# Keys and normed mixer output transposed by DMA instead of TensorE in a hybrid decoder layer

## The chip, the cores and the metric

The kernel runs on the 8 cores of one Trainium2 chip. Each core runs the same program on its own sequence and its own 16 decode requests, and the cores exchange nothing. The metric is the device time of the slowest core in microseconds (us); lower is better. TensorE is called PE, VectorE DVE, ScalarE ACT, GpSimd POOL and SyncE SP.

## What is computed

One decoder layer. Per core: 2048 prompt positions (16 tiles of 128) and 128 sample positions (one tile), model width 1024.

```
z = rmsnorm(h) @ w_in                    # columns u, v_g, q, k, v_m, o, two gates
u, vg = gelu(u), layernorm(gelu(vg))
y_gm = u * (W_s vg + b)                  # causal 128x128 mixing per head, chunks of 128
# mLSTM, 4 heads of 128, chunks of 128:
s   = (q k^T) * w_intra
num = s v + w_inter * (q C);  den = sum(s) + w_inter * (q n)
C   = dec * C + (w_end * k)^T v          # state from chunk to chunk (n alike)
y_ml = sigmoid(o) * rmsnorm(num / max(|den|, exp(-m)))
h = h + concat(y_gm, y_ml) @ w_out
h = h + square(relu(rmsnorm(h) @ w_up)) @ w_down       # width 4096
h = h + sigmoid(rmsnorm(h) @ w_gate) * (p @ w_p)
y = rmsnorm(h)
```

## The kernel before

**Tiles and groups.** The 17 tiles form nine groups: groups 0 to 3 and 5 to 8 are pairs of prompt tiles, group 4 is the sample tile alone. So "from the second pair on" covers 15 tiles. In the order of work the tiles are numbered 0 to 16, the sample tile being number 8.

**Stages of the mixer.** For each group: N normalises and transposes the input (`norm_T`, by PE up to group 4, by DMA from group 5 on), U and V make the two halves of the gMLP, P projects q, k, v, o and the gates (`stage_P`), G works out the gates, M is the mLSTM, the output projection and the residual (`stage_M`). N, U and V of a group run three groups ahead of its P, G and M. Between groups, buffers with index `d2` (keys `KT`, queries `QT`, gates `SGT`) alternate in two places.

**What stage_M does for one tile.** It (1) transposes the scaled keys back to token rows, four 128x128 transposes on PE into one PSUM bank (L1251, L1252), and multiplies them by `wend` into `ktok` (L1253); (2) makes the weights and scores, with keys and queries in feature rows; (3) multiplies scores by values, adds the part from the carried state, and updates the state with `ktok`; (4) normalises, which leaves `yml` in token rows; (5) transposes `yml`, again four on PE into PSUM (L1301, L1302), gates it into `yt` (L1304), and (6) does the output projection from `ut` and `yt`, whose result DVE adds to the residual row in SBUF. Eight early tiles are then stored in DRAM (`hscr`) and loaded again for the FFN.

**FFN and the rest.** The FFN runs in four quarters over its width (B0 to B3), each over six groups of up to three tiles. Its weights come in halves from GpSimd's DMA queue (`load_q`): w_up of the first quarter goes where w_u and w_v stood, w_down where w_m and w_o stood. After them the parked tiles are loaded and then the second quarter's weights. Its inputs are normalised by `norm_B`: the first two groups' transposes by PE, the others' by DMA, through two buffers `AB` taken by turns. The sample's state update and the last stage (C) run beside the later quarters.

**What sets the order.** The program is first listed as operations with their dependences, and a planner (`Plan.schedule`, L449) deals them to the engines: with modelled durations it takes, for each engine, the operation that can start first, and among those within 0.02 us the lowest rank. Ranks come from due times and are moved by hand-kept offsets, `MOVES` (L585): a stage, a stage on an engine, or one operation by number. Each engine then executes its list in order, and waits on semaphores. All DMA transposes are issued by SP, in order with its loads and stores (`Emit.dma`, L258; L276 is the issue itself). All computing instructions are recorded on one line, L252, so that groups are told apart by shapes and names. Nearly all SBUF tiles lie in one tensor, AR; PSUM banks are pb; the identity is IDB.

Of the kernel before, what the change touches and what calls it, by code (L numbers as in the profile page):

```python
# [7 lines left out]
AF = mybir.ActivationFunctionType  # L8
ALU = mybir.AluOpType
# [573 lines left out]


MOVES = """  # L585
B0 -569  B1/pe 15.2  B1 55.2  B2/pe 70.2  B2 52.7  B3/pe 31.8  B3 36.9  C/pe 13.2  C/dve 106.1  G0 -74.9
G2/dve -13.1  G2 -22  G3 -13.4  G4/pe 11.5  G4/act 31.6  G4 -25.1  G5/dve 2.2  G6/dve 47.4  G6 -39.7  G8/dve -15.3
G8 16.9  M0/act -52  M0 -48.5  M1/pe -7.4  M1/dve 19.4  M1 -14.6  M2/pe -3.2  M2 -14.5  M3/pe 19.2  M3/dve 4.9
M3/pool 2  M4/pe -41.2  M4 41.4  M5 -83.3  M6/pe -5.1  M6 -1.3  M7/pe 10.5  M7/act 5.8  M7/dve 6.5  M7 18.5
M8/pe -18.6  M8/act 36.3  M8 10.7  N1/dve 2.2  N1 30.7  N2 22.1  N4 -8.2  P0/act -7.4  P0 -83.9  P1/pe -2.9  # L590
P1 -15.8  P2/pe 22.8  P2 -20.1  P3/pe 21.6  P3 -40.7  P4/pe 0.8  P4 4.6  P5 -10.5  P6/pe -3.3  P6 -7.2  P7/pe -7.8
P7/act -16.5  P7 37.8  P8 59  SU/pe -15.2  SU 187.8  U3/pe -27.2  U3 17.7  U8 -4.8  V1/pe -13.9  V1 28  V2/pe -15.5
V2/dve -26.5  V2 15  V3/pe -33.1  V3 33.3  V4 -12.6  V5/pe -18.8  V5/act 21  V5 -31.6  V6 56  V7/pe -33.8  V7 -13.5
V8 175  #52 -2.7  #54 -4.2  #55 -0.4  #72 11.6  #101 -9.3  #119 -8.9  #120 -4  #144 22.6  #153 -5.2  #158 -11.1
#179 -21.3  #184 -6.5  #190 -20.8  #226 15.9  #235 -6.5  #237 -14.5  #261 -12.6  #275 -34.8  #294 -1.1  #295 -0.2
#310 4.8  #312 8.4  #316 1.8  #324 18  #332 14  #337 -10.2  #340 -3.2  #343 -6.5  #357 -11.6  #358 -19.4  #389 7.2
#415 14.6  #416 4.4  #426 -2.8  #427 -12  #432 -7.5  #443 9.1  #479 20.9  #494 -7.3  #501 1.5  #504 -4.4  #506 -7.7
#537 -13.7  #563 -5.2  #582 -2.8  #585 -8.3  #586 5.1  #591 14.5  #592 -25.8  #593 16.4  #602 -8.9  #635 45.4
#636 14.5  #661 4.8  #669 25.7  #675 12.9  #681 10.4  #696 -26.3  #732 32.4  #747 -8.5  #755 5.6  #756 4.6
#763 28.4  #766 -22.3  #780 -17.5  #781 14.2  #790 -2  #791 -3.5  #808 -3.9  #811 19.4  #821 -2.8  #844 -14.3  # L600
#858 9.8  #873 28.2  #909 -19.4  #912 20.1  #919 -4.1  #921 -8.4  #923 -5.9  #925 -22.8  #934 -8.6  #939 -35.3
#940 14.2  #953 -5.3  #978 -30.6  #999 14.9  #1001 -8.6  #1026 7.1  #1028 0.7  #1071 -30  #1072 -3.5  #1075 17.7
#1078 3.6  #1080 12.3  #1083 -21.1  #1085 21.8  #1088 -13.1  #1092 33.2  #1102 6.3  #1107 -10.7  #1110 6
#1112 -15.3  #1113 -21.1  #1122 16.4  #1134 -13.5  #1136 -7.5  #1173 -15.8  #1181 -26.7  #1200 -1.8  #1202 2.6
#1204 1.6  #1205 -3  #1207 17.1  #1213 -0.9  #1215 -4.6  #1225 -17.1  #1231 -2.4  #1232 1.4  #1236 -0.4  #1247 4.1
#1254 -3  #1268 19.9  #1292 16  #1296 9.9  #1297 23.1  #1316 6.5  #1330 -25.5  #1337 18.4  #1340 -25  #1390 -15.6
#1399 2.1  #1420 -5.4  #1421 -4.5  #1434 -6.9  #1436 35.6  #1439 13.6  #1446 9.7  #1448 -29.9  #1450 -7.5
#1456 18.5  #1461 10.6  #1480 -6.4  #1486 16.7  #1491 20.6  #1495 -2.5  #1549 19.2  #1558 -1.5  #1562 -5.9
#1571 13.8  #1642 -15.4  #1667 39  #1717 62.2  #1753 -28.9  #1807 -10.3  #1825 28.6  #1852 9.3  #1855 -19
#2054 79.2  #2070 -7.6  #2083 23  #2115 -33.1  #2118 12.1  #2189 -21.1  #2198 -15.6  #2322 29.9  #2477 44.4  # L610
#2521 28.5  #2523 8.5  #2525 -19  #2538 22.6  #2555 -15.4  #2557 -14.7  #2617 128.9  #2621 73.4  #2663 33.3
#2703 42.9  #2757 43.2  #2759 65.2  #2781 -3.2  #2799 13.4  #2801 17.5  #2825 58.9  #2838 41.1  #2865 -35.9
#2881 30.5  #2901 27.1  #2923 18.3  #2940 -12.3  #2977 -39.5  #2999 -83.9  #3001 37.8  #3006 -35.4  #3023 118
#3048 -9.3  #3050 -55  #3065 -116.3
"""

DM = 1024
# [9 lines left out]
def build():  # L627
# [35 lines left out]
    with ExitStack() as st:  # L663
# [9 lines left out]
        def psb(cls):  # L673
            return V(PT(cls), PBB[0][:, :], True)
# [12 lines left out]
        def act(out, in_, func, bias=None, scale=None, accum=None):  # L687
            kw = dict(out=out, in_=in_, func=func)
            if bias is not None:
                kw["bias"] = bias  # L690
            if scale is not None:
                kw["scale"] = scale
            if accum is not None:
                kw["accum_out"] = accum
            cost = 0.17 + _nelem(in_) / 1200.0 + 0.09 * nptr(bias, scale) + (0.19 if accum is not None else 0)
            return P.add("act", [("activation", kw)], aps(in_, bias, scale), aps(out, accum), cost, tset=FN.get(func))
# [25 lines left out]
        def stt(eng, out, in0, scalar, in1, op0, op1):  # L722
            return P.add(eng, [("scalar_tensor_tensor", dict(out=out, in0=in0, scalar=scalar, in1=in1, op0=op0,
                                                             op1=op1))],
                         aps(in0, scalar, in1), [out], vcost(eng, _nelem(out), 1, nptr(scalar)))
# [43 lines left out]
        def trs(items):  # L769
            calls, reads = [], []  # L770
            for (o, i_, d_) in items:
                calls.append(("transpose", dict(out=o, in_=i_, identity=d_)))
                reads += [i_, d_]
            return P.add("pe", calls, reads, [items[0][0]], (0.056 if _dsize(items[0][1].dtype) == 2 else 0.109) * len(items))
# [89 lines left out]
        AT[0] = A.bf(8 * 256, k8(8))  # L864
        UT[3] = A.bf(4 * 256, h4)
        UT[0] = A.bf(4 * 256, h4)
        SGT, QT, KT = [[A.bf(4 * 256, h4) for _ in range(2)] for _ in range(3)]
        VAUG = [A.bf(4 * 130, h4)[:, :, 0:129] for _ in range(4)]
        BIG = [A.f32(512, h4) for _ in range(2)]
        STB = [A.bf(512, h4) for _ in range(2)]  # L870
# [72 lines left out]
        def vaug(t):  # L943
            return VWS[:, :, 0:129] if t["ty"] else VAUG[t["n"] % 4]
# [101 lines left out]
        def feat(nm, at, n, fin):  # L1046
            for hp in range(2):
                w, o_ = win(nm, hp)
                p = ps("P")
                for hh in range(2):  # L1050
                    mm(p[:, hh * n:(hh + 1) * n],
                       [(w[:, kc, o_ + hh * 128:o_ + hh * 128 + 128], at[:, kc, 0:n]) for kc in range(8)])
                fin(p[:, 0:2 * n].rearrange("p (h t) -> p h t", h=2), slice(hp * 2, hp * 2 + 2))
# [51 lines left out]
        def stage_P(gi):  # L1105
            grp = GROUPS[gi]
            n = len(grp) * 128
            at = AT[gi % NAT]
            d2 = gi % 2
            pg = ps("P")  # L1110
            mm(pg[0:64, 0:n], [(WGT[:, kc, :], at[:, kc, 0:n]) for kc in range(8)])
            feat("o", at, n, lambda p, hs: act(SGT[d2][:, hs, 0:n], p, AF.Tanh, scale=0.5))
            for j, t in enumerate(grp):
                cp("act", vaug(t)[:, :, 0:128], tokm("m", at, j).rearrange("p (h d) -> p h d", h=4))
            feat("q", at, n, lambda p, hs: cp("act", QT[d2][:, hs, 0:n], p))
            feat("k", at, n, lambda p, hs: act(KT[d2][:, hs, 0:n], p, AF.Copy, scale=QK_SCALE))
            return pg

        def stage_G(gi, pg):
# [119 lines left out]
        def stage_M(gi, gs):  # L1239
# [4 lines left out]
            for j, t in enumerate(grp):  # L1244
# [1 line left out]
                tk = slice(j * 128, (j + 1) * 128)  # L1246
                wint, emt, wend = ex[:, j, 0, :], ex[:, j, 1, :], ex[:, j, 2, :]
                big = BIG[n % 2]
                va, kt, qt = vaug(t), KT[d2], QT[d2]
                ktok = KTOK[n % 2] if ty == 0 else KTOKS[:]  # L1250
                pk = psb("M")  # L1251
                trs([(pk[:, h * 128:(h + 1) * 128], kt[:, h, tk], IDB[:]) for h in range(4)])  # L1252
                tt("dve", ktok, pk[:, 0:512].rearrange("p (h d) -> p h d", h=4),  # L1253
                   wend.unsqueeze(2).to_broadcast([128, 4, 128]), ALU.mult)
                pc = ps("M").rearrange("p (h t) -> p h t", h=4)
                mmx([(pc[:, h, :], OH[:, h, :], r3[:, tk], True, True) for h in range(4)])
                tt("dve", big, pc, MSK[:, ty, :].unsqueeze(1).to_broadcast([128, 4, 128]), ALU.add)
                for h in range(4):
                    act(big[:, h, :], big[:, h, :], AF.Exp, bias=aat[:, j, h:h + 1])
                psc = ps("M").rearrange("p (h t) -> p h t", h=4)  # L1260
                mmx([(psc[:, h, :], kt[:, h, tk], qt[:, h, tk], True, True) for h in range(4)])
                stb = STB[n % 2]
                tt("dve", stb, psc, big, ALU.mult)
                num, qcs = NUM[n % 2], QCS[n % 2] if ty == 0 else QCSS
# [11 lines left out]
                if ty == 0:  # L1276
# [21 lines left out]
                tt("pool", rq, tq, NEGH[:, 0:4], ALU.pow)  # L1298
                yml = YML[n % 2]
                tt("dve", yml, num[:, :, 0:128], rq.unsqueeze(2).to_broadcast([128, 4, 128]), ALU.mult)  # L1300
                py = psb("M")  # L1301
                trs([(py[:, h * 128:(h + 1) * 128], yml[:, h, :], IDB[:]) for h in range(4)])  # L1302
                yt = yml
                stt("dve", yt, SGT[d2][:, :, tk], 1.0, py[:, 0:512].rearrange("p (h t) -> p h t", h=4),  # L1304
                    ALU.add, ALU.mult)
                for nn in range(2):
                    cs = slice(nn * 512, (nn + 1) * 512)
                    ph = ps("M")
# [316 lines left out]
```

How the kernel before makes its waits and increments, by code:

```python
    def _emit_waits(self, eng, toks):  # L229
        for t in toks:
            if t.key[0] == "d":
                sem, val = self._sem(t.key), t.val
            else:
                sem, val = self._eng_sem_val(t.key[1], t.val)
            self.prog[eng].append(lambda e, sem=sem, val=val: e.wait_ge(sem, val))
# [13 lines left out]
        def run(e, calls=calls, sem=sem):  # L249
            ins = None
            for (name, kw) in calls:
                ins = getattr(e, name)(**kw)
            ins.then_inc(sem, 1)
# [4 lines left out]
    def dma(self, eng, kw, out, in_, after=()):  # L258
        deps, rr, wr = self._deps_for([in_], [out], "dma")
        deps += after
        i = self.dma_i[eng]
        self.dma_i[eng] += 1
        skey = ("d", eng, i % NDMASEM)
        prev = self.dma_last.get(skey)
        if prev is not None:
            deps.append(prev)
        self._emit_waits(eng, self._waits(eng, deps))
        val = self.dma_cnt.get(skey, 0) + 16
        self.dma_cnt[skey] = val
        sem = self._sem(skey)
        clock = dict(self.knows[eng])
        clock[skey] = val
        tok = Tok(skey, val, clock)
        self.dma_last[skey] = tok
        self.prog[eng].append(
            lambda e, out=out, in_=in_, sem=sem, kw=kw: e.dma_start(out=out, in_=in_, **kw).then_inc(sem, 16))
        self._record(rr, wr, tok, "dma")
        return tok
```

## Time and profile before

| | |
|---|---|
| median of 3 runs | 892.16 us (890.17 to 940.5) |
| profiled execution | 891.83 us |
| its span, slowest core | 890.3 us (cores: 880.0 to 890.3) |
| mean granted PE clock, that core | 0.989 |
| PE / DVE / ACT / POOL busy | 96% / 61% / 45% / 23% |

The span runs from the first to the last instruction of the core. A matmul's listed duration is that from its start to its result, and neighbours overlap; PE's time per matmul is the distance between starts.

### The profile page before, as it was taken

To read this page: it belongs to the slowest core of one execution; us is meant where nothing else is said; L and a number is where in the kernel's file an instruction comes from. 1 tells how busy PE (TensorE), PEld (TensorE's weight loads), DVE (VectorE), ACT (ScalarE), POOL (GpSimd) and SP (SyncE) were. 2 spreads that over 40 slices of the span, in tenths; PEclk is the share of its full clock that TensorE was granted. 3 is DMA by queue.
4 is the path that set the end of the run, shared out by engine and by line. 5 is a ranking of instruction groups with operands and counts; after the bars stand their busy time and mean duration, and the time that the engine had idled before them with its cause. 6 is when DMAs were issued, how large, how long until landed. Compare 5 with 4: busy or idle time off the path is not lost.

```text
span 890.3 us, 16667 instructions; the slowest of 8 cores (880.0 to 890.3 us)
## 1 busy us (share of the span) xinstructions
PE 856.0 (96%) x5650; PEld 513.1 (58%) x5650; DVE 539.9 (61%) x1080; ACT 398.4 (45%) x776; POOL 203.5 (23%) x312
## 2 busy tenths in 40 slices
PE   3989999999999999889999999999999999999995
PEld 2658666877677755445655555655556545455452
DVE  5858787486876884454544445755544544665566
ACT  2866567766675654351221121211122244645454
POOL 4334224425443242110010000211000011312211
PEclk9999999999999999989999999999999999999999
DMA  8995234125123079851192011682102523432322
GB/s 195 205 182 98 96 119 108 49 49 119 25 49 61 8 116 261 136 103 66 48 142 49 1 48 48 103 181 78 35 24 35 107 50 77 125 89 81 89 69 95
DMA packets 66821, 80.57 MB, mean 91 GB/s; under 512 B 43132, under 2 KB 45440, under 8 KB 65458
## 3 DMA queue, kind: packets, MB, share of 16 engines
q0 software_dynamic: 13648, 32.71, 21.9%
q1 hardware_dynamic: 53090, 46.80, 18.8%
q8 instruction: 47, 0.77, 0.4%
q14 instruction: 36, 0.29, 0.1%
HBM read 81.23 MB, written 18.12 MB: 112 GB/s over the span
## 4 chain that ended last, share of the span: by engine, by line
PE 86%; DMA 6%; ACT 2%; issue 2%; SPq 1%; DVE 1%; POOL 1%; POOLq 0%; ACTq 0%; DVEq 0%
PE pb L252 86%; DMA AR<-AR 3%; ACT AR L252 2%; DMA AR<-w_down 1%; SPq L276 1%; DVE AR L252 1%; DMA AR<-w_u 1%; DMA AR<-xp 1%; POOL SMALL L252 1%; ACT L252 0%; POOLq L283 0%; DVE SMALL L252 0%; ACTq L235 0%; DVEq L235 0%; SPq L235 0%
## 5 line engine op out<-in xcount | busy, mean ns | idle before, releaser
L252 PE MATMUL pb<-AR 128*128 128x512 bf16 (+6 forms) x5280 | 842.2, 320 | 10.2 <-DVE AR L252 6.5
L252 PEld LDWEIGHTS pb<-AR 128*128 128x128 bf16 (+2 forms) x5280 | 488.9, 99 | 343.9 <-issue 24.5
L252 ACT ACTIVATE AR<-pb 128x384 f32<-128x384 f32 (+4 forms) x356 | 171.8, 494 | 372.5 <-PE pb L252 306.5
L252 DVE TENSOR_TENSOR AR<-AR,pb 128x512 f32<-128x512 f32 (+3 forms) x226 | 132.6, 591 | 122.6 <-PE pb L252 122.0
L252 DVE TENSOR_TENSOR AR<-AR 128x384 bf16<-128x384 f32 (+7 forms) x257 | 136.0, 533 | 109.4 <-ACT AR L252 100.7
L252 ACT ACTIVATE AR<-AR 128x1024 bf16<-128x1024 f32 (+7 forms) x178 | 114.2, 674 | 65.4 <-DVE AR L252 35.3
L252 POOL TENSOR_TENSOR SMALL<-SMALL,NEGH 128x1 f32<-128x1 f32 (+1 forms) x102 | 70.1, 691 | 43.2 <-DVE SMALL L252 33.2
L252 POOL TENSOR_SCALAR SMALL<-SMALL 128x1 f32<-128x1 f32 x84 | 25.3, 301 | 236.8 <-ACT AR L252 206.7
L252 ACT ACTIVATE AR<-AR,SMALL 128x1024 bf16<-128x1024 f32 (+1 forms) x61 | 63.1, 1043 | 28.9 <-POOL SMALL L252 20.2
L252 DVE TENSOR_TENSOR AR<-pb,AR 128x258 f32<-128x258 f32 (+3 forms) x86 | 47.6, 580 | 17.2 <-PE pb L252 14.3
L252 POOL TENSOR_TENSOR AR<-AR 128x512 bf16<-128x512 f32 (+2 forms) x37 | 44.6, 1210 | 53.8 <-ACT AR L252 48.7
L252 DVE SCALAR_TENSOR_TENSOR AR<-AR,pb 128x512 f32<-128x512 f32 (+1 forms) x51 | 34.7, 684 | 31.0 <-PE pb L252 26.9
L252 POOL TENSOR_TENSOR AR<-KTOKS,CPK 128x1024 bf16<-128x1024 bf16 x8 | 15.3, 1912 | 163.7 <-PE pb L252 163.7
L252 DVE TENSOR_TENSOR AR<-AR,CPK 128x1024 bf16<-128x1024 bf16 (+3 forms) x29 | 25.4, 877 | 20.4 <-DMA AR<-AR 20.2
L252 DVE TENSOR_TENSOR AR<-pb,CPK 128x512 f32<-128x512 f32 (+2 forms) x33 | 29.7, 912 | 10.0 <-PE pb L252 9.8
L252 PE MATMUL pb<-IDB,AR 128*128 128x128 bf16 x272 | 23.5, 225 | 11.9 <-DVE AR L252 11.8
L252 POOL CAST AR<-AR 128x256 bf16<-128x256 f32 (+1 forms) x33 | 19.3, 586 | 51.5 <-DMA o_Cs<-AR 20.6
L252 PEld LDWEIGHTS pb<-IDB,AR 128*128 128x128 bf16 x272 | 18.9, 100 | 15.8 <-issue 12.6
L252 ACT ACT_TABLE_LOAD x20 | 25.7, 1283 | 3.9 <-PE pb L252 2.3
L252 DVE SCALAR_TENSOR_TENSOR AR<-AR,SMALL 128x1024 f32<-128x1024 f32 (+1 forms) x17 | 21.3, 1255 | 8.7 <-POOL SMALL L252 8.6
L252 ACT ACTIVATE AR<-pb,AR 128x129 f32<-128x129 f32 (+1 forms) x68 | 20.3, 368 | 12.9 <-PE pb L252 12.8
L252 DVE SCALAR_TENSOR_TENSOR AR<-AR 128x1024 f32<-128x1024 f32 (+3 forms) x27 | 24.5, 910 | 1.8 <-DVE AR L252 0.5
(72 smaller groups left out, 198.5 us busy)
## 6 DMA issues: line engine op xcount, KB each, us to landing
AR<-w_up POOLq DMA_DIRECT2D x8, 1024.0 KB, 11.1
AR<-w_down POOLq DMA_DIRECT2D x8, 1024.0 KB, 11.4
y_p<-AR SPq DMA_DIRECT2D x15, 512.0 KB, 2.6
hscr<-AR SPq DMA_DIRECT2D x8, 512.0 KB, 3.9
AR<-xp SPq DMA_DIRECT2D x4, 1024.0 KB, 5.2
AR<-hscr SPq DMA_DIRECT2D x8, 512.0 KB, 6.9
AR<-sC SPq DMA_DIRECT2D x8, 512.0 KB, 4.9
o_Cs<-AR SPq DMA_DIRECT2D x8, 512.0 KB, 3.5
```

What stands on the lines that cost most here:

```text
L252: ins = getattr(e, name)(**kw)
L276: lambda e, out=out, in_=in_, sem=sem, kw=kw: e.dma_start(out=out, in_=in_, **kw).then_inc(sem, 16))
```

## The change

For groups 1 to 8 the keys are transposed by one DMA of 128x512 into `ktok`, which DVE then multiplies in place by `wend`. The output `yml` is transposed by another DMA into the place of the tile's keys, and gated there. The key buffer holds each tile's keys in one run (tile, head, position), where before the two tiles of a pair lay side by side within each head. Group 0 stays on PE. The list of priority offsets is replaced as a whole (its first lines stand below).

```diff
 MOVES = """
-B0 -569  B1/pe 15.2  B1 55.2  B2/pe 70.2  B2 52.7  B3/pe 31.8  B3 36.9  C/pe 13.2  C/dve 106.1  G0 -74.9
...
+B1/pe 41.2  B1 111  B2/pe 76.6  B2 90.7  B3/pe 43.2  B3/dve -52  B3 21.6  BN1 453.9  C/pe 3.2  C/dve -57.6  C 20.3
...
-        SGT, QT, KT = [[A.bf(4 * 256, h4) for _ in range(2)] for _ in range(3)]
+        SGT, QT = [[A.bf(4 * 256, h4) for _ in range(2)] for _ in range(2)]
+        KT = [A.bf(4 * 256, ("p (j h t) -> p h j t", dict(j=2, h=4))) for _ in range(2)]
...
-            feat("k", at, n, lambda p, hs: act(KT[d2][:, hs, 0:n], p, AF.Copy, scale=QK_SCALE))
+            feat("k", at, n, lambda p, hs: act(KT[d2][:, hs, 0:n // 128, :], p.rearrange("p h (j t) -> p h j t", t=128),
+                                               AF.Copy, scale=QK_SCALE))
...
-                va, kt, qt = vaug(t), KT[d2], QT[d2]
+                va, kt, qt = vaug(t), KT[d2][:, :, j, :], QT[d2]
                 ktok = KTOK[n % 2] if ty == 0 else KTOKS[:]
-                pk = psb("M")
-                trs([(pk[:, h * 128:(h + 1) * 128], kt[:, h, tk], IDB[:]) for h in range(4)])
-                tt("dve", ktok, pk[:, 0:512].rearrange("p (h d) -> p h d", h=4),
-                   wend.unsqueeze(2).to_broadcast([128, 4, 128]), ALU.mult)
+                if gi:
+                    dma(ktok, kt.rearrange("p h t -> p (h t)"), transpose=True)
+                    ksrc = ktok
+                else:
+                    pk = psb("M")
+                    trs([(pk[:, h * 128:(h + 1) * 128], kt[:, h, :], IDB[:]) for h in range(4)])
+                    ksrc = pk[:, 0:512].rearrange("p (h d) -> p h d", h=4)
+                tt("dve", ktok, ksrc, wend.unsqueeze(2).to_broadcast([128, 4, 128]), ALU.mult)
...
-                py = psb("M")
-                trs([(py[:, h * 128:(h + 1) * 128], yml[:, h, :], IDB[:]) for h in range(4)])
-                yt = yml
-                stt("dve", yt, SGT[d2][:, :, tk], 1.0, py[:, 0:512].rearrange("p (h t) -> p h t", h=4),
-                    ALU.add, ALU.mult)
+                if gi:
+                    ysrc = yt = kt
+                    dma(yt, yml.rearrange("p h d -> p (h d)"), transpose=True)
+                else:
+                    py = psb("M")
+                    trs([(py[:, h * 128:(h + 1) * 128], yml[:, h, :], IDB[:]) for h in range(4)])
+                    ysrc, yt = py[:, 0:512].rearrange("p (h t) -> p h t", h=4), yml
+                stt("dve", yt, SGT[d2][:, :, tk], 1.0, ysrc, ALU.add, ALU.mult)
```

## Rows read from the trace of the kernel before

**Rows 1.** The page: the span, and busy time of each engine

```profile
span 890.3 us, 16667 instructions; the slowest of 8 cores (880.0 to 890.3 us)
...
PE 856.0 (96%) x5650; PEld 513.1 (58%) x5650; DVE 539.9 (61%) x1080; ACT 398.4 (45%) x776; POOL 203.5 (23%) x312
```

**Rows 2.** Waits of PE, whole run: us in total, times, longest us

```profile
PE pb L252 <- DVE AR L252: 21.3, 9, 10.9
```

**Rows 3.** Waits of PE from 49 to 310 us

```profile
PE pb L252 <- DVE AR L252: 2.8, 2, 2.6
```

**Rows 4.** Timeline of PE, three stretches: start us, us, operation, count, idle before

```profile
208.63 0.39 PE L252 MATMUL pb<-IDB,AR 128*128 128x128 bf16 x4
208.86 3.05 PE L252 MATMUL pb<-AR 128*128 128x129 bf16 x36
...
329.45 28.28 PE L252 MATMUL pb<-AR 128*128 128x384 bf16 x152
...
380.70 24.58 PE L252 MATMUL pb<-AR 128*128 128x384 bf16 x123 [5.77 <-DVE AR L252]
```

**Rows 5.** The chain that ended last, in order of time: start us, us

```profile
49.04 123.76 PE pb L252 x1085
...
318.88 12.42 DMA AR<-w_down
...
343.30 9.03 DMA AR<-AR
...
369.44 9.79 DMA AR<-AR
```

**Rows 6.** Windows, PE: us, busy (instructions), granted clock, DMA share, GB/s

```profile
170.00:180.00 10.00, 9.81 (x88) 1.00 0.29 54
350.00:360.00 10.00, 9.82 (x58) 1.00 1.09 159
376.00:381.00 5.00, 0.30 (x2) 0.67 0.61 83
381.00:384.00 3.00, 3.00 (x11) 0.50 0.09 5
```

**Rows 7.** Groups, shapes apart: PE's transposes (busy us, mean ns, idle before)

```profile
L252 PE MATMUL pb<-IDB,AR 128*128 128x128 bf16 x272 | 23.5, 225 | 11.9 <-DVE AR L252 11.8
```

**Rows 8.** Groups, shapes apart: keys by weights, output scaled, gating, power

```profile
L252 POOL TENSOR_TENSOR SMALL<-SMALL,NEGH 128x4 f32<-128x4 f32 x17 | 18.4, 1087 | 31.6 <-DVE SMALL L252 31.5
...
L252 DVE SCALAR_TENSOR_TENSOR AR<-AR,pb 128x512 bf16<-128x512 bf16 x17 | 11.6, 684 | 3.7 <-PE pb L252 3.7
L252 DVE TENSOR_TENSOR AR<-AR,SMALL 128x512 bf16<-128x512 f32 x17 | 11.6, 681 | 1.6 <-POOL SMALL L252 1.6
...
L252 DVE TENSOR_TENSOR AR<-pb,AR 128x512 bf16<-128x512 bf16 x16 | 10.8, 686 | 2.1 <-PE pb L252 1.4 <-ACT AR L252 0.5
```

**Rows 9.** L276, SP's issues: ns min/median/max; then SP's timeline near 330 us

```profile
L276 SPq DMA_TRANSPOSE AR<-AR x51: 1168/1233/6755, 113.9 to 860.1; - x51
...
326.85 2.14 SPq L276 DMA_TRANSPOSE AR<-AR  x1
335.29 6.75 SPq L276 DMA_TRANSPOSE AR<-AR  x1
```

**Rows 10.** DMA transposes, us to landing: 130 to 160 us, 165 to 250, 310 to 360

```profile
AR<-AR SPq DMA_TRANSPOSE x2, 5.2
...
AR<-AR SPq DMA_TRANSPOSE x4, 3.1
...
AR<-AR SPq DMA_TRANSPOSE x5, 9.6
```

**Rows 11.** DVE's timeline, last tile's output scaled and gated: start us, us

```profile
327.63 0.68 DVE L252 TENSOR_TENSOR AR<-AR,SMALL 128x512 bf16<-128x512 f32 x1
...
329.72 0.69 DVE L252 SCALAR_TENSOR_TENSOR AR<-AR,pb 128x512 bf16<-128x512 bf16 x1 [0.33 <-PE pb L252]
```

**Rows 12.** POOL's timeline: the first half of w_down is issued

```profile
307.23 0.83 POOL L276 DMA_DIRECT2D AR<-w_down  x1 [3.59 <-PE pb L252]
```

More of the change, by code:

```diff
@@ L585 @@
 MOVES = """
-B0 -569  B1/pe 15.2  B1 55.2  B2/pe 70.2  B2 52.7  B3/pe 31.8  B3 36.9  C/pe 13.2  C/dve 106.1  G0 -74.9
[L587 to L614, printed above, removed]
+B1/pe 41.2  B1 111  B2/pe 76.6  B2 90.7  B3/pe 43.2  B3/dve -52  B3 21.6  BN1 453.9  C/pe 3.2  C/dve -57.6  C 20.3
+G0 -100.2  G1/act -9.3  G1/dve 55.9  G1 -20.8  G2/pe -10.3  G2/act -36.3  G3 -85.7  G4 -41.4  G6/dve -13.4  G6 -5.8
@@ new lines @@
+G7/act -54.1  G7/dve -22.4  G7 27.4  G8/dve -13.1  M0/pe -14.3  M0 -14.3  M1 -27.2  M2 -47.9  M3/pe 19.1
+M3/act -15.5  M3 16.3  M4/pe -42.9  M4/dve 23  M4 22.7  M5 -161.4  M6/act 9.9  M6 -16.7  M7/pe 23.4  M7/act -11.2
+M7 33.3  M8/pe 36.5  M8/dve 5.6  M8 16.5  N1/dve -24.5  N1 31.5  N7/dve 29.6  N7 -16.7  P0 -41.4  P1/pe -0.9
+P1 -4.3  P2/pe 13.2  P2 -21.9  P3/pe -2.9  P3 -19  P4/pe 18.8  P4 16.7  P5/pe 31.2  P5 21.7  P6/pe 31.1  P7 44.5
+P8 28.4  SU 108.9  U3/pe 11.2  U3 62.2  U4 44.7  U5/pe 15.4  U6/pe -11.5  U6/act 6.3  V0 -46.1  V1/pe -11.5  V1 3.7
@@ new lines @@
+V2/pe -6.8  V2 3.4  V3/pe 2.5  V3/dve 76.7  V3 51.1  V4 76.6  V5/pe -2.2  V5 -3.8  V6 120.2  V7/dve -11.5  V7 -45.6
+V8 78.7  #55 -7.7  #60 37.3  #96 -6.3  #97 -3.4  #120 5.5  #125 23.7  #153 24.8  #173 -12  #195 7.6  #222 -6.3
+#226 8.6  #286 33.8  #288 -16.1  #292 -29.2  #294 25.7  #318 41.7  #325 -34  #357 -0.8  #364 1.6  #365 -12.7
+#394 15.3  #412 31.7  #413 12.9  #416 9.8  #423 3.3  #429 12.3  #432 -11.9  #444 -40.9  #445 3.5  #447 -42.7
+#480 22.3  #496 -8.8  #497 -10  #513 -2.8  #514 -10.7  #522 -2.9  #523 -17.1  #557 35.5  #559 8.6  #588 -15.5
@@ new lines @@
+#590 13.9  #593 -6.9  #617 29.1  #620 -6.4  #622 -14.9  #645 14.4  #647 13.8  #658 15  #659 -40.3  #661 12.8
+#670 -22.2  #681 7.6  #687 29.7  #699 34.9  #727 -13.1  #738 15  #747 -0.4  #758 14  #760 -7  #765 -9.9  #766 -8.3
+#771 -0.2  #776 -17.9  #782 -22.3  #787 43.2  #790 11.1  #797 16.3  #819 10.9  #822 11  #828 -36.4  #841 15.3
+#860 59.6  #869 17.8  #887 -22.6  #892 -20.9  #905 17.2  #920 7.4  #922 -5.4  #923 -8.4  #926 -4.9  #930 13
+#931 8.9  #933 -15.2  #934 -1.5  #936 -15  #937 -15  #939 -11  #940 -5.3  #944 -6.8  #957 13.2  #960 -28.2
@@ new lines @@
+#961 -8.4  #967 4.9  #1001 -23.7  #1022 6.1  #1069 7.1  #1071 -9.6  #1076 -3  #1083 -10.2  #1085 -15.1  #1088 5
+#1092 -8.3  #1110 -6.4  #1111 -8.1  #1173 -12.6  #1205 -3.1  #1210 14.3  #1212 -5.7  #1216 7.2  #1219 5.3
+#1225 10.3  #1234 21.4  #1299 -12.3  #1332 -20.6  #1336 -19.9  #1343 32  #1358 -23.2  #1359 22.9  #1361 -10.9
+#1364 21.5  #1380 -23.7  #1381 -12.1  #1385 -6.3  #1414 -21.6  #1425 20  #1442 16.7  #1445 14.5  #1452 15.2
+#1453 -5.3  #1454 22.6  #1459 6.1  #1461 -15.3  #1466 -15.2  #1475 19  #1479 20.5  #1489 25.7  #1495 5.9  #1501 21
@@ new lines @@
+#1505 1.3  #1517 12.6  #1518 6.4  #1526 22.6  #1544 13.1  #1590 -29.9  #1626 43.1  #1633 3.3  #1650 -36.4
+#1665 81.5  #1667 -23.8  #1717 46.3  #1867 30.7  #1890 20.9  #1986 25.6  #2014 32  #2039 53.5  #2058 48.8
+#2095 12.1  #2158 23.6  #2201 64.4  #2217 37.6  #2276 11.2  #2407 42  #2409 -23.3  #2439 21.7  #2449 13.5
+#2482 -5.8  #2487 -23.1  #2518 -48.7  #2519 -33.1  #2521 -14.1  #2523 48.8  #2527 79.7  #2538 -53.6  #2541 53.1
+#2557 34.4  #2561 10.7  #2563 6.1  #2577 -22.2  #2599 11.5  #2637 9.5  #2640 50.4  #2661 7.5  #2665 72.5
@@ L615 @@
+#2699 -10.2  #2701 -4.5  #2719 -102.7  #2721 31.9  #2739 -5.2  #2745 -49.5  #2751 -6.7  #2765 25.9  #2781 -68
+#2783 -21.7  #2805 -40.5  #2825 -57.1  #2847 3.3  #2861 -15.6  #2879 6.5  #2885 10.7  #2923 -52.6  #2925 -50.8
+#2929 -83.3  #2979 87.4  #3001 -6.2  #3005 -68.7  #3021 18.4  #3026 34.6  #3046 -81.1  #3061 -5.3
 """
@@ L1260, in stage_M @@
                 psc = ps("M").rearrange("p (h t) -> p h t", h=4)
-                mmx([(psc[:, h, :], kt[:, h, tk], qt[:, h, tk], True, True) for h in range(4)])
+                mmx([(psc[:, h, :], kt[:, h, :], qt[:, h, tk], True, True) for h in range(4)])
                 stb = STB[n % 2]
```

## The prediction

> **What bounds the kernel now.** I read the page first. TensorE (PE) is busy for 856.0 of 890.3 us, and no other engine passes 61% [rows 1]. So 34.3 us of PE idleness are all that better overlap could give, and beyond that only less PE work helps. The waits of PE say where the idleness is: 21.3 us behind VectorE (DVE) in nine places, the longest of 10.9 us at the very start, where DVE makes the identity; the rest of the 34.3 is the loads at the start and the tail after PE's last matmul [rows 2]. In the 261 us from 49 to 310 us, which hold nearly all of the mixer, PE waits for DVE only 2.8 us [rows 3]. The mixer is therefore bound by PE's stream of instructions: what leaves that stream there leaves the time, as long as nothing arrives late. The one gap inside the run that matters is the passage from mixer to FFN: PE stands still for 5.77 us before 380.70, released by DVE [rows 4]. The chain of waits shows what was late there [rows 5]: a half of w_down lands at 318.88 + 12.42 = 331.3, the parked tiles are loaded, and then three DMA transposes of normed FFN tiles, 9.0 to 9.8 us each (the first and the last stand there), follow one behind the other, because two buffers (AB) serve them by turns. DMA is jammed there: its share is 1.09 from 350 to 360 us [rows 6].
>
> **The removed PE work.** From group 1 on there are 15 tiles; each loses four transposes of the keys and four of the normed output, 120 of the 272 transposes of 128x128 bf16 in the whole run [rows 7]. What one costs has two ends. The group's busy time gives 23.5 / 272 = 0.086 us. But a listed matmul has a mean of 225 ns and overlaps its neighbours, so I take the pitch: four start at 208.63 and the next work starts at 208.86 [rows 4]. That is 0.23 us for four, 0.056 to 0.058 us each; other such pairs in PE's timeline stand 0.22 us apart, so I use 0.225. 30 groups of four by 0.225 = **6.75 us** off PE; by busy time it would be 120 x 0.086 = 10.4 us. I take 6.75, since the pitch shows when the next matmul really began; below, the end is 0, if PE merely waits as much longer. Their weight loads lie beside matmuls and count as nothing extra.
> The Trainium skill, "VectorE: DVE Perf Modes", section "The three transpose paths", gives a TensorE transpose of this size 390 ns and the DMA's crossbar 1309 ns, and its "Rules for kernel authors" say to use TensorE wherever a PSUM destination will do, as it would here: a rule against this change. By its 390 ns, the estimated relief would be 46.8 us; the rows' pitch says a seventh of that. The rule enters as the last rival.
>
> **DVE.** No operation is removed. The multiply of the keys by their weights read PSUM at 686 ns and now reads SBUF; its like, the multiply of the mixer output with both sources in SBUF, takes 681 ns. The gating operation with PSUM takes 684 ns [rows 8]; without it I bound the change by 681 and 686, so 0 to within 0.1 us over 30 instructions. Both now have two SBUF sources, which could hold up GpSimd or be held up by it; the nearest thing on POOL is the power of four numbers, 1.09 us each [rows 8]. At worst once per tile, 15 x 1.09 = 16 us of delay, at best none; DVE is busy 61% and PE works on other tiles, so I put 0 on the path.
>
> **The added DMAs.** 30 transposes of 128x512, all from SyncE's queue. One occupies that queue for at least 1.17 us, median 1.23, and at most 6.76 us, in the jam of the passage [rows 9]. All 51 of before include sizes of half and double the new one, so the new ones take some 30 x 1.23 = 37 us of queue. The mixer's nine groups fill PE from 49.0 to 329.5 us [rows 4, 5], 31 us each, 248 us for groups 1 to 8: room enough, since the other issues there are few tens. For the engines: from 170 to 180 us the share is 0.29 and the traffic 54 GB/s [rows 6], which is two 128x1024 transposes and hardly anything else (0.54 MB), so 1.45 us of all 16 engines each and 0.73 for half the size. 30 x 0.73 = 22 us over 248, nine points of share on top of a low load outside the weight loads.
> The Trainium skill, "Advanced Engine Details and Errata", section "X-Bar Transpose (TRN2)", expects 350 to 400 GB/s and transposes as fast as plain DMAs. By that the estimated load is about half, 10 us in place of 22. The row has 0.256 MB in 1.45 us, some 180 GB/s, and decides.
>
> **The added latency.** A transpose takes 3.1 us from issue to landing in a quiet stretch, 5.2 where it meets other traffic, and 9.6 in the passage [rows 10]. Before, the way over PE cost less: the last tile's output is scaled at 327.63 + 0.68 and gated at 329.72, 1.4 us later [rows 11]. So a tile's output projection comes 2 us later at rest and up to 8 us later in a jam.
> Keys: they are ready long before their use in the state update, and the transpose is not in the chain of the state; 0. Outputs: the front of the work runs three groups ahead, so PE has projections of other tiles to do; the 2.8 us of waits in 261 say that such work is never short [rows 3]. I put 0 there for groups 1 to 7, with 15 x 2 = 30 us as the far end if each tile waited. If that cover is gone, nothing but the last group remains, and there the cover ends: group 8 (tiles 15 and 16 in order of work) has no further group behind it, only FFN work on early tiles.
> Waits on SP: what queues behind a transpose waiting for the scaled output are stores of parked tiles, loads of x and later transposes of normed inputs, none wanted for tens of us, except at the end: the eight loads of parked tiles. They wait for w_down's landing at 331.3 anyway [rows 5]; the last output is ready at 328.3. Margin: 3.0 us, against a normal hold of 1.23. I take 0, and 6.76 for one held hard.
> Buffers: the output takes over the keys' place, which is then free one output projection later. Its next writer is the key projection two groups on; a group takes some 31 us; 0. The key layout is only an address pattern; 0. Freed PSUM banks can only help; 0.
>
> **The passage.** Its chain starts with w_down, whose first half is issued at 307.23 when PE has done its last use of the room [rows 12], the second at 318.88 [rows 5], behind the power of tile 15 in POOL's order. Both follow PE's progress, and by then 28 of 30 groups of transposes are gone: the chain starts 6.3 us earlier. So I let the gap stay at 5.8 and the gain pass through.
>
> **New priorities.** They move every start, and the trace of before can't price them. PE idleness in the mixer leaves at most 2.8 us to win; the passage 5.77 us, and the clock behind it: granted 0.67 from 376 to 381 and 0.50 from 381 to 384 [rows 6], where PE worked at 1.2 instead of 2.4 GHz, at 0.50 for 3 us, so 1.5 us of work lost. Together 7.3 can be won there. As much can be lost by a like gap elsewhere. I take 0.
>
> **Sum.** The profiled execution took 891.83 us, 1.5 more than its span; 891.8 - 6.75 = 885.1. The median of before, 892.16, lies 0.3 above the profiled run: 885.4.
>
> **Rivals.**
> 1. *The passage closes as well.* FFN normalisation of the second group gets its own late place, which may free ACT and AB for the tiles that were late; PE's gap and the half clock go. 885.4 - 7.3 = 878. For it: three serial 9 us transposes are a matter of order. Against: DMA is full there, and order moves no bytes.
> 2. *The gain is absorbed.* PE reaches the passage 6.75 us earlier but the tiles wait for DMAs that don't come earlier, or the added latency at the tail of the mixer eats it. 892. For it: the chain there is DMA. Against: its start is released by PE.
> 3. *Slower: SyncE's queue jams at the tail.* The output transposes of tiles 15 and 16 meet the load of w_down and hold the queue 6.76 us each, and the loads of parked tiles stand behind them. 2 x 6.76 = 13.5, less the 6.3 by which the chain starts earlier = 7.2 later than before; the gap is longer and the clock falls for longer (another 1.5): 892.2 + 8.7 = 901. It decides from a hold of more than 3.0 us for the last one. For it: holds of 6.75 appear from 335 us on. Against: at 326.85 one still went through in 2.14 [rows 9].
> 4. *The way over DMA is too long for every tile*: a 2 us wait of PE at each of 15 tiles, 30 us less 6.75, gives 885.4 + 30 = 915. For it: the added latency of 2 us is certain. Against: PE's waits of 2.8 us in the mixer [rows 3]. This is what following the rule of "VectorE: DVE Perf Modes" in the Trainium skill would avoid.
> That the change doesn't do what it says is also possible: the added DMAs could leave PE's order such that removed transposes had filled time in which it waited for DVE anyway; this is case 2 by another way.
>
> **Chances.** Forecast (881 to 889) 0.49, passage closed 0.16, absorbed 0.19, queue jam 0.12, too slow 0.04. The range reaches below the closed passage and short of the jam's full price, 876 to 900, which leaves out about 2 in 10. A change of 2%, 17.8 us, is about what a measurement of this kernel tells from none. Below 874.3 would need the closed passage and more: 0.04. Above 910 needs case 4 or a doubled jam: 0.05. Within: 0.91.
>
> **What would show it.** PE's transposes drop from 272 to 152 and its busy time by 7 to 10 us; DMA transposes rise from 51 to 81; PE's waits from 49 to 310 us stay below 5 us; the gap before the third FFN group stays 4 to 8 us with a dip of the clock behind it; DVE's groups keep 680 to 690 ns; landing of transposes in the mixer is near 3 us outside the loads. The forecast is wrong if PE's waits in the mixer exceed 7 us, if a wait of PE ends on a new DMA transpose at the tail, or if the gap before the FFN's third group changes by more than 4 us.

## The result: no faster, 0.23% slower, and the profile after

Over 20 runs each the changed kernel takes 893.9 us (median) against 891.54; the ratio is 1.0023, 95% interval 1.0014 to 1.0032. The forecast was 885.4, a gain of 0.76%. The gain is absent and the sign is the other one. Some runs of every kernel are slower by several per cent, with a lower clock on some of the cores; the medians count them, the ratios don't.

The page of the changed kernel, against [rows 1]: PE has 7.9 us less to do, and the span is not shorter.

```profile
span 891.2 us, 16401 instructions; the slowest of 8 cores (881.7 to 891.2 us)
...
PE 848.1 (95%) x5464; PEld 508.5 (57%) x5534; DVE 538.6 (60%) x1080; ACT 399.8 (45%) x778; POOL 205.2 (23%) x312
```

Groups with shapes apart, against [rows 7, 8]: PE's transposes, the gating from SBUF, the keys by their weights from SBUF.

```profile
L252 PE MATMUL pb<-IDB,AR 128*128 128x128 bf16 x152 | 12.9, 232 | 12.0 <-DVE AR L252 12.0
...
L252 DVE SCALAR_TENSOR_TENSOR AR<-AR 128x512 bf16<-128x512 bf16 x15 | 10.2, 681 | 0.0
L252 DVE TENSOR_TENSOR AR<-AR 128x512 bf16<-128x512 bf16 x14 | 9.4, 689 | 2.9 <-DMA AR<-AR 2.9
```

So 120 transposes left PE and DVE pays nothing for its new operands. PE's waits from 49 to 310 us are another matter; before there were 3.0 us, 2.8 of them behind DVE [rows 3], now 7.5, more than the 7 at which the prediction calls itself wrong:

```profile
PE pb L252 <- DVE AR L252: 3.1, 1, 3.1
PE pb L252 <- ACT AR L252: 3.0, 1, 3.0
PE pb L252 <- POOL AR L252: 0.8, 2, 0.4
PE pb L252 <- issue: 0.6, 3, 0.2
```

PE's timeline says where, and that PE still stands still in the passage from mixer to FFN, now in three pieces of together 6.2 us instead of one of 5.77 [rows 4]:

```profile
64.08 12.49 PE L252 MATMUL pb<-AR 128*128 128x129 bf16 x120 [3.03 <-ACT AR L252]
...
303.82 4.22 PE L252 MATMUL pb<-AR 128*128 128x129 bf16 x20 [3.13 <-DVE AR L252]
...
356.56 4.08 PE L252 MATMUL pb<-AR 128*128 128x384 bf16 x16 [2.22 <-DVE AR L252]
...
381.50 4.44 PE L252 MATMUL pb<-AR 128*128 128x384 bf16 x16 [2.33 <-DVE AR L252]
387.63 12.90 PE L252 MATMUL pb<-AR 128*128 128x512 bf16 x63 [1.69 <-DVE AR L252]
```

The new one in the mixer is the wait before 303.82. The chain in order of time leads through a DMA transpose to a DVE operation; DVE's timeline has there the keys' multiply of the last tile:

```profile
293.03 9.86 DMA AR<-AR
302.89 0.03 issue
302.94 0.04 issue
302.98 0.70 DVE AR L252
303.68 0.14 issue
303.82 1.45 PE pb L252 x12
```

SyncE's timeline: four transposes (the keys of tiles 15 and 16, the outputs of 13 and 14) hold its queue for 19 us, while POOL issues the first half of w_down.

```profile
288.28 19.09 SPq L276 DMA_TRANSPOSE AR<-AR  x4
```

```profile
292.28 0.83 POOL L276 DMA_DIRECT2D AR<-w_down  x1 [1.84 <-PE pb L252]
```

The transposes' us to landing, first from 60 to 285 us, then from 286 to 310:

```profile
AR<-AR SPq DMA_TRANSPOSE x31, 2.8
...
AR<-AR SPq DMA_TRANSPOSE x4, 7.6
```

And the windows of PE (stretch, its length, busy us and instructions, granted clock, DMA share, GB/s): the stretch with the wait has a mean granted clock of 0.66 where the one before it has 1.00. From 304 to 310 us, right behind the wait, PE is at work at 0.50, so the 3.1 us cost more than themselves.

```profile
290.00:300.00 10.00, 9.55 (x102) 1.00 0.66 98
300.00:310.00 10.00, 6.59 (x29) 0.66 1.07 133
```

### The profile page after: what moved, and what is told of

Read it like the earlier page. It is cut to its first block, busy times and chain, and to the rows that moved or that the text cites. A ratio compares the mean times of both kernels' runs of the same rounds, so it can differ in the third digit from the quotient of the medians.

```text
span 891.2 us, 16401 instructions; the slowest of 8 cores (881.7 to 891.2 us)
## 1 busy us (share of the span) xinstructions
PE 848.1 (95%) x5464; PEld 508.5 (57%) x5534; DVE 538.6 (60%) x1080; ACT 399.8 (45%) x778; POOL 205.2 (23%) x312
## 4 chain that ended last, share of the span: by engine, by line
PE 82%; DMA 11%; issue 2%; POOL 2%; ACT 2%; DVE 1%; SPq 0%; POOLq 0%; ACTq 0%; DVEq 0%
PE pb L252 82%; DMA AR<-AR 6%; DMA AR<-xp 3%; ACT AR L252 2%; DMA AR<-xs 1%; DVE AR L252 1%; POOL SMALL L252 1%; DMA CPK<-cpk 1%; POOL AR L276 0%; POOL AR L252 0%; SPq L276 0%; POOLq L283 0%; POOL CPK L276 0%; ACTq L235 0%; POOLq L235 0%
## 5 line engine op out<-in xcount | busy, mean ns | idle before, releaser
L252 PE MATMUL pb<-AR 128*128 128x256 bf16 (+6 forms) x5210 | 835.3, 320 | 21.9 <-DVE AR L252 9.8
L252 PEld LDWEIGHTS pb<-AR 128*128 128x128 bf16 (+1 forms) x5280 | 490.9, 99 | 354.7 <-issue 31.8
L252 ACT ACTIVATE AR<-pb 128x384 f32<-128x384 f32 (+6 forms) x356 | 172.1, 494 | 362.2 <-PE pb L252 285.0
L252 DVE TENSOR_TENSOR AR<-AR 128x384 bf16<-128x384 f32 (+9 forms) x271 | 140.7, 524 | 105.6 <-ACT AR L252 99.1
L252 ACT ACTIVATE AR<-AR 128x1024 bf16<-128x1024 f32 (+6 forms) x178 | 113.8, 675 | 89.0 <-DVE AR L252 51.8
L252 DVE TENSOR_TENSOR AR<-pb,AR 128x512 bf16<-128x512 f32 (+3 forms) x72 | 38.5, 559 | 13.9 <-PE pb L252 12.8
L252 DVE SCALAR_TENSOR_TENSOR AR<-AR,pb 128x512 f32<-128x512 f32 (+1 forms) x36 | 24.5, 684 | 23.1 <-PE pb L252 22.5
L252 DVE SCALAR_TENSOR_TENSOR AR<-AR 128x1024 f32<-128x1024 f32 (+4 forms) x42 | 34.7, 827 | 1.4
L252 PE MATMUL pb<-IDB,AR 128*128 128x128 bf16 x152 | 12.9, 232 | 12.0 <-DVE AR L252 12.0
L252 DVE SCALAR_TENSOR_TENSOR AR<-AR,DECBS,pb 128x128 f32<-128x128 f32 x64 | 19.9, 343 | 1.8 <-PE pb L252 1.8
```

The costliest lines, as they stand in the source:

```text
L252: ins = getattr(e, name)(**kw)
```

## The experiments

Each is given as its ratio to the kernel of before, run beside it on the same chip, with the 95% interval.

**The list and the transposes apart.** Two runs exchange the lists of offsets, `MOVES`; one puts group 8 back on PE and one leaves the transposes out, and both are planned anew.

```diff
e1_old_list:        the change, MOVES of before
e2_new_list_alone:  before, MOVES of the change
e3_last_group_pe:
-                if gi:
+                if 0 < gi < 8:
e4_no_transpose (the numbering of operations kept for MOVES):
-                    dma(ktok, kt.rearrange("p h t -> p (h t)"), transpose=True)
-                    ksrc = ktok
+                    ksrc = kt
-                    ysrc = yt = kt
-                    dma(yt, yml.rearrange("p h d -> p (h d)"), transpose=True)
+                    ysrc, yt = yml, kt
```

> The change with the priority list of before. Theory J (the DMA path is late in the last group and in the passage, whatever the order): within 3 us of the change, about 890 to 897, with a wait of PE of some 3 us behind a key or output transpose at the end of the mixer. Rival L (the new list costs what the change gains): faster than before, 884 to 887, with PE's waits in the mixer back under 1 us. If the list was fitted to the change, more than 897.

> The kernel of before with the new priority list, all transposes on PE. Theory J: a list that fits another kernel, so 892 to 900, but no wait of PE on a transposing DMA before 310 us. Rival L: the list alone brings the early gap at 61 us and the gap near 300 us, and the time is 6 to 9 us over before, 898 to 901.

> The change, but group 8 (the last two tiles) transposes on PE again: 16 of the 120 transposes come back, 0.9 us of PE. Theory J: the wait of 3.1 us before 303.8 and the half clock behind it go, so 3 to 5 us faster than the change net of 0.9: 888 to 891 on a median of 893.9. Rival L: no gain, 893 to 896.

> The change with the transposes of groups 1 to 8 left out altogether: keys are weighted and outputs gated untransposed, by the same DVE operations (so the results of these groups are of untransposed data). It prices the relief of PE alone. Theory J: all of the 6.75 us shows and part of the passage's gap remains: 883 to 887 against 891.5 of before. Rival R (PE's relief is worth little, since PE is held up in the passage anyway): 889 to 892. Rival L: 889 to 894.

Measured: 1.0303 (1.0282 to 1.0323), 1.0258 (1.0244 to 1.0271), 1.0058 (1.0043 to 1.0074) and 1.0302 (1.0283 to 1.0321). With the list of before, the changed kernel has PE idle in many small places; its window of PE, whose like in the kernel of before has 240.8 us busy in 241:

```profile
49.00:290.00 241.00, 228.63 (x1880) 0.96 0.48 95
```

None of the four answers its question. Each list is fitted to one kernel: e1, e2 and e4 lose 23 to 27 us against the kernel of before, even e4, which only leaves work out. e3, which differs from the change in group 8 alone, is some 3 us slower than the change, where theory J wanted 3 to 5 us less; that may be its own plan too. What they show is this: the list belongs to the change, and no part can be tried by planning again. From here on the plan is made as in the kernel named, and the edit is applied afterwards (`MOD` is true then), with every engine's instructions left in their order and every PSUM bank where it was:

```diff
+        for o in P.ops:
+            r = ref.ops[o.idx]
+            o.fill = r.fill
+            for p, q in zip(o.pts, r.pts):
+                p.bank = q.bank
+        order = [P.ops[r.idx] for r in ref.order]
```

**What is PE's relief worth, and what do the DMAs cost?** f4 is before without the 120 PE transposes; f1 is the change without its 30 DMAs. f3 holds w_down back in the change; g2 gives the FFN's transposes a third buffer.

```diff
f4_before_order_no_transpose (gi > 0; the trs operations aren't issued):
+                    ksrc = kt[:, :, tk]
+                    ysrc = yml
f1_order_kept_no_dma (the dma operations aren't issued):
+                    ksrc = kt
+                    ysrc = kt
f3_w_down_after_keys:
+            q0[2].after = list(q0[2].after) + k8_      # landings of group 8's key transposes
g2_after_three:
-                norm_T(t["n"], 44, Hs(t), AB[t["n"] % 2], ...
+                    ab = (AB + [AB3])[nb_[0] % 3]
```

> The kernel of before in its own order, only the 120 transposes of groups 1 to 8 on PE not issued (keys weighted and outputs gated untransposed, from SBUF). Prices PE's relief with nothing added. By the pitch: 891.5 - 6.75 = 884.8 if the passage moves along; rival A (the passage and the chains of other engines absorb it): 887 to 891.

> The change with every engine's instructions in the order of the change, word for word, only the 30 added DMAs not issued (keys are weighted and outputs gated in place, untransposed). Theory J (late transposes give the gain back): no wait near 300 us, hscr loads and FFN transposes earlier, 884 to 888 against 891.5 of before and 893.9 of the change. Rival O (the order of the new list, its early gap at 61 us above all, costs it): 892 to 894, the gaps at 61 and in the passage stay.

> The change in its own order, but the first half of the first w_down load is issued only when the key transposes of group 8 have landed. Theory J: those transposes land in about 3 us, the wait of 3.1 us before 303.8 and its half clock go, w_down comes some 2 us later: 889 to 892. Rival: w_down's delay is handed on to the passage one for one, or the wait moves to the next transpose: 893 to 896.

> The change in its own order, with a third buffer for the FFN inputs that are transposed by DMA (groups 3 to 6 of the FFN), so that three transposes of 10 us can be in flight instead of two. Theory P (the passage is a chain of buffer and latency): its waits of 2.2, 2.3 and 1.7 us shrink by half or more, 887 to 891. Rival D (the passage is bound by DMA bandwidth): transposes just take 15 us each, 893 to 895.

f4: 0.9953 (0.9940 to 0.9966). The relief alone brings 0.47%, 4.2 us (3.0 to 5.3), of the 6.75. PE's timeline of f4 shows small waits that weren't there before, and the gap of the passage not shorter:

```profile
71.83 10.23 PE L252 MATMUL pb<-AR 128*128 128x129 bf16 x106 [0.67 <-ACT AR L252]
141.57 9.69 PE L252 MATMUL pb<-AR 128*128 128x512 bf16 x56 [0.81 <-DVE AR L252]
...
376.49 43.71 PE L252 MATMUL pb<-AR 128*128 128x384 bf16 x220 [6.09 <-DVE AR L252]
```

f1: 0.9967 (0.9954 to 0.9980), between both theories' ranges: 2.9 us below before and 5.0 below the change. So the DMAs cost 0.56%, more than the relief brings. The wait of 3.03 at 64 us belongs to the order (f1 still has 2.56 there); that order isn't clearly worse than the old one, since the intervals of f1 and f4 overlap.

f3: 1.0032 (1.0020 to 1.0044), no gain. The hold sits in POOL's queue; PE's long wait for the keys is gone, but one of 1.9 us for a small DVE operation and 1.6 us for POOL take its place. It doesn't tell the theories apart.

g2: 1.0096 (1.0065 to 1.0127), slower. PE stands once for 10.62 us. The transposes from 318 to 400 us land in a median of 6.4 us, against 7.6 in the change, so the 15 us of rival D don't show either; why PE stands longer wasn't traced. What the run shows is that a third buffer doesn't shorten the passage.

**Which of the DMAs?** All in the order of the change; each leaves some DMAs out (keys or outputs untransposed there), except k2, which does those of groups 7 and 8 on PE.

```diff
f2_no_last_keys:    keys of group 8 left out
m1_no_late_outputs: outputs of groups 7 and 8 left out
h1_no_late_dma:     keys and outputs of groups 7 and 8 left out
h2_no_early_dma:    keys and outputs of groups 1 to 6 left out
k2_last_pe:
+                    if MOD and (gi >= 7):
+                        pk = psb("M")
+                        late_.append([trs([(pk[:, h * 128:(h + 1) * 128], kt[:, h, :], IDB[:]) for h in range(4)])])
...
```

> The change in its own order, without the two key transposes of group 8 (its keys are weighted untransposed). Theory K (the late key transpose, landing at 302.9, makes the 3.1 us wait and the half clock): the wait near 303.8 is gone and 3 to 5 us come back, 889 to 891 where the change has 894. Rival B (the passage takes back whatever arrives early): under 2 us, 892 to 894.

> The change in its own order, without the eight transposes of groups 7 and 8 (keys and outputs untransposed there). If the late ones are the whole price of the DMAs: as without any DMA, 889 to 890. If rival S holds (every transpose in the mixer costs PE something, by shares of DMA and waits): 892 to 893.

> The counterpart: without the 22 transposes of groups 1 to 6, those of groups 7 and 8 stay. If the late ones are the whole price: 893 to 895, as the change. Rival S: 890 to 892.

> The change in its own order, but the eight groups of four transposes of groups 7 and 8 back on PE, each just before its use, all else untouched: 1.8 us of PE come back. Theory K: no wait near 300 us, so the change's 894 less 5 plus 1.8 = 890 to 892, faster than before by a little. Rival B: 893 to 896, the passage keeps it.

> The change in its own order without the four output transposes of groups 7 and 8 (outputs gated untransposed there), their key transposes stay. The eight together cost 0.47% (0.9976 to the change's 1.0023), the two last keys alone 0.1%. If the outputs are the larger part: 890 to 891.5. If it is the keys of group 7 or only all together: 892.5 to 894.

| run | DMAs left | ratio | 95% interval |
|---|---|---|---|
| the change | 30 | 1.0023 | 1.0014 to 1.0032 |
| h2 | the 8 late ones | 1.0032 | 1.0017 to 1.0046 |
| m1 | 26 | 1.0023 | 1.0012 to 1.0034 |
| f2 | 28 | 1.0013 | 1.0004 to 1.0022 |
| h1 | the 22 early ones | 0.9976 | 0.9965 to 0.9987 |
| k2 | the 22 early ones | 0.9973 | 0.9962 to 0.9984 |
| f1 | none | 0.9967 | 0.9954 to 0.9980 |

The 22 early ones cost nothing that can be measured (h1 against f1, the change against h2). Not all of them ran in quiet: in the change two, between 234 and 258 us, went beside a load of w_up and landed in a median of 6.0 us, and PE, busy 34.8 of the 35 us from 230 to 265, waited for neither. So a slow landing costs nothing while PE has other tiles' work.

The eight late ones cost 0.47%, 4.2 us (the change against h1); with the early ones left out it is 0.65% (h2 against f1). They cost it together: without the two last keys 0.1% comes back, without the four outputs nothing. The traces say why one kind alone is enough. In m1, where the keys stay, PE waits 3.83 us near 306, as in the change. In f2, where the outputs stay, the wait for the keys is gone and another has come, with a mean granted clock of 0.66 from 315 to 320 us behind it; h1, without either kind, has neither:

```profile
314.49 7.90 PE L252 MATMUL pb<-AR 128*128 128x512 bf16 x32 [1.99 <-DVE SMALL L252]
```

So the wait of 3.13 us isn't by itself the price, and how the price is shared between keys and outputs stays open. k2 is the change made useful: with the eight back on PE it is 0.50% faster than the change, at 889.83 us and 0.27% below the kernel of before. The end of its mixer has no wait above 0.6 us, but the passage keeps its gaps:

```profile
354.40 20.92 PE L252 MATMUL pb<-AR 128*128 128x384 bf16 x112 [0.48 <-DVE AR L252]
378.54 4.08 PE L252 MATMUL pb<-AR 128*128 128x384 bf16 x16 [3.22 <-DVE AR L252]
384.44 13.12 PE L252 MATMUL pb<-AR 128*128 128x512 bf16 x64 [1.83 <-DVE AR L252]
```

**The passage.** In every kernel so far the second quarter's weights are loaded as soon as the parked tiles are in. In the kernel of before they are issued from 346 to 382 us, and PE is done with the first quarter's w_up only at 445, some 60 to 100 us later. The FFN's input transposes share DMA with them. These runs hold the loads until a transpose has landed.

```diff
p1, p2, p3 (on k2, before, the change): until the fifth FFN group's last transpose
r1, r2 (on k2, before): until the sixth group's last transpose, with the state loads that stood before it moved behind it
+        q1_[0].after = list(q1_[0].after) + [land_]
-            dma(CSF[c % 3], sC[h, :, half * 8:half * 8 + 8, :], after=q1[3:])
+            dma(CSF[c % 3], sC[h, :, half * 8:half * 8 + 8, :], after=())
```

> The kernel of before in its own order, all transposes as there, but the second quarter's FFN weights (4 loads) and the first state loads don't wait for each other any more, and the first of these weight loads is issued only when the fifth FFN group's last input transpose has landed. Theory Q (the passage stands still because the FFN transposes share DMA with weights that are needed 70 us later): the transposes land in 3 to 5 us instead of 9, the wait of 5.8 us and the half clock go, 884 to 887. Rival W (the weights then come too late for the second quarter, or the chain of two buffers holds anyway): 891 or more, with a wait of PE on w_up near 445 us.

> The same hold on the change in its own order. Theory Q: the waits of 2.2, 2.3 and 1.7 us in the passage go, what the late transposes cost before 318 us stays: 886 to 890. Rival W: 893 or more.

> The change with groups 7 and 8 transposed on PE and the hold. Theory Q: both gains add up, 889.8 less 4 to 7: 883 to 886, faster than both kernels. Rival W: 890 or more.

p2 1.0097 (1.0083 to 1.0111), p3 1.0101 (1.0086 to 1.0117), p1 1.0071 (1.0058 to 1.0083): all slower, and yet the theory holds where the hold holds. In p2 PE has no gap above 0.3 us between 318 and 399, and the transposes there land in a median of 3.1 us instead of 8.8. The whole stand is now behind the two transposes that were left outside the hold. They are issued at 382.65 and 384.21, among the four weight loads (377.10 to 383.67) and right behind them, and in the chain the second takes 26 us:

```profile
384.21 26.05 DMA AR<-AR
```

```profile
415.07 17.45 PE L252 MATMUL pb<-AR 128*128 128x512 bf16 x78 [15.81 <-DVE AR L252]
```

> The kernel of before with the hold stretched over the sixth group's two transposes too; two or three state loads come after them. In the shorter hold PE's gaps from 318 to 400 us were gone, but these two transposes met the weights and PE stood for 15.8 us. Theory Q: without that wait 900.7 less 15.8 and less about 1.5 of half clock, 883 to 886. Rival W (now the weights are late for the second quarter): 889 or more, with a wait of PE on w_up or w_down between 430 and 450 us.

> The change with groups 7 and 8 on PE and the stretched hold. Theory Q: 898.7 less 14.9 less 1.5, 880 to 884, the fastest of all. If the passage no longer takes anything back, it should lie 4 to 5 us below the kernel of before with the same hold. Rival W: 889 or more.

r2, the kernel of before with the longer hold: 882.64 us, 0.9910 (0.9896 to 0.9924). r1, the repaired change with it: 881.19 us, 0.9889 (0.9874 to 0.9905). Windows of PE with clock, DMA share and GB/s, of before, r2 and r1 in this order:

```profile
318.00:400.00 82.00, 76.00 (x415) 0.95 0.81 155
```

```profile
318.00:400.00 82.00, 81.42 (x456) 1.00 0.61 136
400.00:450.00 50.00, 49.84 (x294) 1.00 0.69 119
```

```profile
318.00:400.00 82.00, 81.62 (x450) 1.00 0.44 108
400.00:450.00 50.00, 49.84 (x296) 1.00 0.80 132
```

In r2 PE is busy 5.4 us more of the 82 than before, and at full clock. The second quarter's weights, now issued from 388 us on and landed by about 430, still come in time. r1 lies in its range and r2 just below its own, but they are 0.2% apart, not the 4 to 5 us expected, and their intervals overlap.

The gap of the passage differs from core to core, and the time is that of the slowest. In the profiled execution of before it was 1.71 us on core 3, whose span was 880.0 us, and 5.77 on core 6 with 890.3. In r2 no core has a gap above 0.3 us there, and the spans are 877.7 to 880.8 us. So what the hold gives is for the most part that the slow cores come up to the fast ones.

## Why the prediction was wrong, by its own steps

**The removed PE work** was right: 120 transposes less, PE's busy time down by 7.9 us. That all of it arrives was not. Alone it brings 4.2 us (f4), so **the sum** overstated this term by 2.6. A part went in the step "by then the chain starts 6.3 us earlier": in f4 POOL issues the first half of w_down at 303.66 instead of 307.23, 3.6 us earlier. That execution began the mixer 0.9 us later (PE's wait there ends at 49.98 instead of 49.04), where the two kernels are still the same, so by the trace some 4.5 us had arrived. Waits of 0.67 and 0.81 us that weren't there before make up most of what is missing; later ones of 0.78 and 0.55, and a gap of 6.09 for 5.77, come on top.

**DVE** and **the added DMAs** in the quiet mixer were right: 681 to 689 ns, landing in 2.8 us, and the early 22 are free (h1 against f1). Rival 4 is excluded. For a 128x128 transpose, "VectorE: DVE Perf Modes" in the Trainium skill, section "Rules for kernel authors", says to use TensorE where PSUM will do as destination. Here the runs are divided on it: for the 22 early ones the DMA cost PE nothing (h1 against f1), for the eight late ones the advice was right, by 0.50% (k2 against the change).

**The added latency** is the step that failed. It gave the keys 0, because they are ready long before their use, and the last outputs 0, for a margin of 3.0 us against a normal hold of 1.23. In the last two groups a key transpose landed after 9.86 us beside w_down's load, and DVE, then PE waited for it 3.13 us, with a clock of 0.66 behind. The measured term, for the eight transposes of these groups together, is 4.2 us where the sum had 0. The step had costed the jam for outputs (5 to 9.6 us, [rows 10]) and had not asked the same of the keys of the same tiles, which go through the same queue at the same time. It also took the queue's load from the order of before, where the first half of w_down is issued at 307.23 [rows 12]; the new order issues it at 292.28, among four of the transposes. Even in the order of before the margin was thin: PE transposed the keys of tiles 15 and 16 there only 0.7 us ahead of that load, and a DMA that needs 3 us would have met it.

```profile
306.52 0.61 PE L252 MATMUL pb<-IDB,AR 128*128 128x128 bf16 x8
```

No run has the added DMAs in the order of before, so what the eight would cost there stays open.

**Rival 3** had the right mechanism, SyncE's queue jammed at the tail of the mixer, and 0.12; it named outputs and the loads of parked tiles, and 901 for a price. The runs give all eight transposes together 4.2 us, and their sum with 4.2 of relief is nought, which is rival 2's number, 892. The remaining 2 us are, by the frozen runs, 1.2 for the order (f1 against f4) and 0.8 for the 22 early DMAs (h1 against f1); in both pairs the intervals overlap, so neither is shown to be more than nothing.

**The passage** was taken to move along unchanged. Its gaps stayed, 6.2 us for 5.77, as the step said. That it could be closed by order was doubted ("order moves no bytes"), and this was wrong: p2, r2 and r1 show that the gap came from which bytes go first. The loads move unchanged, only later. The prediction also laid the serial transposes to the two buffers; with a third one (g2) the passage got no shorter.

**New priorities** at 0: the list's value for its own kernel can't be told from zero, but its bond to that kernel is 2.6 to 3.0%.

## What to carry to other kernels

Here a DMA transpose in place of PE's was free as long as PE had other tiles' work, beside a weight load too. It cost time at the end of the mixer, where it landed after up to 9.86 us instead of 2.8 and that work ran out. So price it per place, by the traffic and the cover at its own time in the new order, and let those that have neither quiet nor cover stay on PE. When a stage waits for small DMAs, look first at which large loads run beside them and when these are needed; holding four weight loads back (by 8 to 42 us in r2) gave more here, 0.9%, than the whole change was meant to. With a schedule fitted by hand, test parts in a frozen order, never by planning again.

## What the runs showed that was not expected

A transpose that usually lands after 2.8 us took 9.86 beside one weight load and 26.05 when it was issued right behind four. A third buffer for such transposes made the kernel 0.7% slower than the change. Leaving work out of a kernel with a fitted list made it 3% slower (e4), when its plan was made again. In one and the same execution the cores of before differ by 10 us, and the gap of the passage goes with it.
